# Heads of a gated recurrence as a pipeline of two, and an output product begun with seven of eight tiles

## The reference, cut to what matters

```python
def lru_coeffs(u2, p):                       # per head of 128 channels, two directions
    gr, gi = u @ w_r, u @ w_i                # 128x128 matrices per head and direction
    r, i = sigmoid(gr + b_r), sigmoid(gi + b_i)
    log_a = -8 * r * softplus(-lam)
    return exp(log_a), sqrt(-expm1(2 * log_a)) * (i * u)     # a, bx

def rglru_branch(xb, p, h0):
    u = depthwise_conv(xb, sconv_w, sconv_b)                 # 4 taps
    y = scan forward (h = a*h + bx) + scan backward, both from h0
    return y, last states

def even_mixer(h, h0, p):                    # D_MODEL 1024, 512 positions
    va, vg, ga, xb, gb = split(h @ w_in)
    y_a = silu(layernorm(depthwise_conv(va * sigmoid(vg), 31 taps))) * silu(ga)
    y_b = rglru_branch(xb, p, h0) * silu(gb)
    return concatenate([y_a, y_b]) @ w_out
```

## Time and profile before

| what | value |
|---|---|
| median of 3 runs | 1792.26 us (1791.04 to 1792.68) |
| the profiled execution's own time | 1792.62 us |
| its span, first to last instruction | 1791.3 us |
| PE busy | 1673.2 us (93%) |
| DVE busy | 992.5 us (55%) |
| ACT busy | 746.1 us (42%) |
| share of PE in the chain that ended last | 71%; DVE 14%, ACT 10%, issue 4% |

### The profile page before, as it was taken

The page is one execution under the profiler, slowest core; times in us unless marked ns, Lnnn a source line. Parts: engine busy times, 40 slices in busy tenths (PEclk is TensorE's granted clock), DMA queues, the critical chain, the costliest instruction groups (busy, mean ns, idle before and its releaser), DMA issues.

```text
span 1791.3 us, 19102 instructions
## 1 busy us (share of the span) xinstructions
PE 1673.2 (93%) x7670; PEld 1297.0 (72%) x7670; DVE 992.5 (55%) x1362; ACT 746.1 (42%) x1014; POOL 19.4 (1%) x40
## 2 busy tenths in 40 slices
PE   6798899996997999999799989999999999999996
PEld 4677666664785888888587857776677788888885
DVE  4677768777757556744744453345545544444333
ACT  3567665765434333332334444334433322332221
POOL 0000000000000000000000000000000000000000
PEclk9799999998998999999899989999999999999998
DMA  7345536454231233232132111221122233232321
GB/s 315 117 159 182 190 129 202 150 178 154 71 106 59 94 97 104 91 100 94 46 111 69 67 47 55 77 70 56 62 94 95 83 102 98 95 94 94 106 94 47
DMA packets 55063, 190.46 MB, mean 106 GB/s; under 512 B 7328, under 2 KB 7328, under 8 KB 54720
## 3 DMA queue, kind: packets, MB, share of 16 engines
q1 hardware_dynamic: 47616, 159.52, 27.4%
q0 software_dynamic: 4960, 18.20, 3.1%
q10 hardware_dynamic: 2400, 11.53, 1.6%
HBM read 178.63 MB, written 2.10 MB: 101 GB/s over the span
## 4 chain that ended last, share of the span: by engine, by line
PE 71%; DVE 14%; ACT 10%; issue 4%; ACTq 1%; DMA 0%; DVEq 0%
PE banks L1446 21%; PE banks L1448 21%; PE banks L1447 21%; ACT w_hi L412 2%; PE banks L1693 2%; DVE w_lo L843 2%; DVE u L980 2%; PE banks L1466 1%; ACT aa L504 1%; ACT tr L506 1%; DVE ti L997 1%; DVE tr L1001 1%; DVE tr L1005 1%; ACT tr L499 1%; PE banks L1715 1%
## 5 line engine op out<-in xcount | busy, mean ns | idle before, releaser
L1446 PE MATMUL banks<-h_hi,w_hi 128*128 128x512 f32 x1408 | 561.1, 398 | 24.4 <-DVE h_lo L919 10.3
L1447 PE MATMUL banks<-h_lo,w_hi 128*128 128x512 f32 x1408 | 553.1, 393 | 0.0
L1448 PE MATMUL banks<-h_hi,w_lo 128*128 128x512 f32 x1408 | 552.3, 392 | 0.0
L843 DVE TENSOR_TENSOR w_lo<-raw,w_hi 128x1024 fp32r<-128x1024 f32 x276 | 336.5, 1223 | 295.5 <-ACT w_hi L412 295.1
L412 ACT ACTIVATE w_hi<-raw 128x1024 fp32r<-128x1024 f32 x276 | 288.2, 1050 | 159.2 <-PE banks L1448 147.8
L1446 PEld LDWEIGHTS banks<-h_hi,w_hi 128*128 128x128 f32 x1408 | 266.7, 189 | 102.6 <-issue 34.4
L1448 PEld LDWEIGHTS banks<-h_hi,w_lo 128*128 128x128 f32 x1408 | 267.3, 190 | 56.9
L1447 PEld LDWEIGHTS banks<-h_lo,w_hi 128*128 128x128 f32 x1408 | 267.5, 190 | 53.8 <-issue 0.7
L1446 PE MATMUL banks<-y_hi,w_hi 128*128 128x512 f32 x192 | 76.8, 400 | 5.7 <-ACT gs L716 5.6
L1448 PE MATMUL banks<-y_hi,w_lo 128*128 128x512 f32 x192 | 76.8, 400 | 0.0
L1447 PE MATMUL banks<-y_lo,w_hi 128*128 128x512 f32 x192 | 76.1, 396 | 0.0
(11 more groups left out here) (347 smaller groups left out, 2145.8 us busy)
## 6 DMA issues: line engine op xcount, KB each, us to landing
raw<-weights SPq DMA_DIRECT2D x284, 512.0 KB, 3.5
mraw<-modt POOLq DMA_DIRECT2D x32, 512.0 KB, 4.5
mod<-modw ACTq DMA_DIRECT2D x4, 2048.0 KB, 23.0
rep<-U SPq DMA_DIRECT2D x96, 64.9 KB, 2.7
rep<-U SPq DMA_DIRECT2D x32, 64.8 KB, 2.5
X<-x_in ACTq DMA_DIRECT2D x1, 2048.0 KB, 13.2
out<-X SPq DMA_DIRECT2D x4, 512.0 KB, 2.7
ctx_x<-ctx_in ACTq DMA_DIRECT2D x1, 1024.0 KB, 19.8
```

What stands on the lines that cost most here:

```text
L843: tt(slot(w_lo, c), slot(raw, c), slot(w_hi, c).bitcast(F32), ALU.subtract).then_inc(S["lo"], 1)
L1446: mm(o, wh, r_hi, start=start, stop=False)
L1447: mm(o, wh, r_lo, start=False, stop=False)
L1448: return mm(o, wl, r_hi, start=False, stop=stop)
```

## The change

Roots, scans and outputs of a head move behind the input of the next head. On ACT `head_input` is cut into the copy to `xp` and `head_high` (the split of `u`), `head_roots` of head I-1 stands after the split of the next weight chunk, and the output split is a function of its own. On DVE the order of a main head becomes: the low part of gx, drive of the head before, `convolved`, scans and output of the head before, conv of this head. The first of the two scratch tiles of square roots is no longer `xp` but a part of `yb_lo`'s tile; the context's `u` gets two halves. The 32 conditioning steps are divided as one per context head and three per main head. On PE the first three chunks of yb are begun with seven of the eight tiles, ahead of the sum of `csum` (behind the first), and finished with the eighth afterwards.

```diff
+    o_ybl = p.at
     yb_lo = p("yb_lo", NT * T, F32R)
+    thf = [at(f"thf{i}", T, o_ybl + 2 * K * i) for i in range(NT)]
@@ ACT
-        def head_input(I, w, b):    # xp, then u_hi
+        def head_input(I, w, b):
+            if I: e.wait_ge(S["conv"], I)
+            else: e.wait_ge(S["pad"], 1)
+            fn(xp[:, 2:2 + w], bank(b, w), ACT.Copy).then_inc(S["xp"], 1)
+        def head_high(I, w):
+            e.wait_ge(S["conv"], I + 1)
+            if I: product(gc or gx of head I - 1)
+            fn(u_hi[:, 0:w], u_of(I), ACT.Copy).then_inc(S["uhi"], 1)
@@ ACT, context heads
             head_input(i, TC, 4)
+            head_high(i, TC)
             ahead("vg", i)
+            if i:
+                head_roots(i - 1)
             product("vg", i)
...
             head_gates(i, TC, ...)
-            head_roots(i, TC)
@@ ACT, main heads
             ahead("xb", i)
+            if i:
+                convolved(i - 1)
+            head_roots(NT + i - 1)
             product("xb", i)
             head_input(NT + i, T, 0)
             if i:
-                convolved(i - 1)
+                head_high_out(i - 1)
+            head_high(NT + i, T)
             ahead("gb", i)
...
             ahead("cw", i)
-            head_roots(NT + i, T)
-            e.wait_ge(S["yact"], i + 1)
-            fn(tile(yb_hi, i), u[:, :], ACT.Copy).then_inc(S["ybhi"], 1)
         convolved(NT - 1)
+        head_roots(2 * NT - 1)
+        head_high_out(NT - 1)
@@ DVE, context heads
             ahead("xc", i)
-            head_input(i, TC)
+            if i:
+                head_drive(i - 1, TC)
+            head_conv(i, TC)
             ahead("vg", i)
+            head_low(i, TC)
+            if i:
+                context_scan(i - 1)
             ahead("va", i)
+            conditioning(i)
             e.wait_ge(S["sig"], i + 1)
             product("va", i)
             stt(U ...).then_inc(S["uu"], 1)
             ahead("gc", i)
-            head_drive(i, TC)
-            conditioning(2 * i)
-            head_scan(i, TC, lambda k: 0.0)
-            conditioning(2 * i + 1)
@@ DVE, main heads, after the change
+            ahead("xb", i)
+            head_drive(NT + i - 1, T if i else TC)
+            if i:
+                convolved(i - 1)
+                head_sum(i - 1)        # both scans, their sum, the gate
+            else:
+                context_scan(NT - 1)
+            head_conv(NT + i, T)
+            if i:
+                head_low_out(i - 1)    # yb_lo
+            ahead("gb", i)
+            head_low(NT + i, T)
+            conditioning(NT + 3 * i)
+            stt(tg ...)                # the gate of gb
+            conditioning(NT + 3 * i + 1)
+            ahead("ga", i)
+            ahead("gx", i)
+            conditioning(NT + 3 * i + 2)
+            stt(sga ...)               # the gate of ga
+            ahead("cw", i)
+        head_drive(2 * NT - 1, T)
+        convolved(NT - 1)
+        head_sum(NT - 1)
+        head_low_out(NT - 1)
@@ PE
-        e.wait_ge(S["csum"], NT)
-        feature_sum(0, csum[:, :])
+        def yb_early(f):
+            c = ready("yb", f)
+            if f == 0:
+                e.wait_ge(S["yblo"], NT - 1)
+                e.wait_ge(S["gread"], 2 * NT)
+            blocks(bank(BANK_OF[f]), c, yb_hi, yb_lo, n=KC - 1, stop=False)
+        def yb_late(f):
+            if f == 0:
+                e.wait_ge(S["yblo"], NT)
+            blocks(..., b0=KC - 1, k0=KC - 1, n=1, start=False, stop=False).then_inc(S["mm"], 1)
         for f in range(3):
-            yb(f)
+            yb_early(f)
+            if f == 0:
+                e.wait_ge(S["csum"], NT)
+                feature_sum(0, csum[:, :])
+        for f in range(3):
+            yb_late(f)
         e.wait_ge(S["usum"], NT - 1)
         feature_sum(1, ti[0][:, :])
```

More of the change, by code:

```diff
@@ L124 @@
     "vec x ctx cst cst2 out hi lo mm crep csb mdv v a zero eps pad sil sp_z sp_e wdt rows cols rows_c x_sum x_sq fsum f_sq "
[L125 removed]
+    "norm_t norm_hi norm_lo xp conv uhi ulo gread e2 mv sq scan sig uu "
     "tgt sgb sgat sga cpe csum yact ybhi yblo ymu usum usq yln ysil yga yhi yalo res xsq xsum "
@@ L357, in program, with u_of, th_of @@
     xg = (sqb[:, :], s2[:, :])
+    def u_of(I):
+        return u[:, :] if I >= NT else tile(u, I % 2, TC)
+    def th_of(I, k):
+        return (thf[I % NT], th[1])[k][:, 0:T if I >= NT else TC]
     def sp():
@@ L488, in head_input @@
                 product(*(("gc", I - 1) if I <= NT else ("gx", I - NT - 1)))
-            fn(u_hi[:, 0:w], u[:, 0:w], ACT.Copy).then_inc(S["uhi"], 1)
+            fn(u_hi[:, 0:w], u_of(I), ACT.Copy).then_inc(S["uhi"], 1)
         def head_gates(I, w, gates):
-            if I:
+            if I > NT:
+                e.wait_ge(S["yblo"], I - NT)
+            elif I:
                 e.wait_ge(S["scan"], I)
@@ L530, in convolved, with head_high_out @@
             fn(tile(U, i, T, UW), bank(3), ACT.Identity, bias=cb2[:, i:i + 1]).then_inc(S["cpe"], 1)
+        def head_high_out(i):
+            e.wait_ge(S["yact"], i + 1)
+            fn(tile(yb_hi, i), tr[0][:, :], ACT.Copy).then_inc(S["ybhi"], 1)
         for i in range(NT):
             ahead("xb", i)
+            if i:
+                convolved(i - 1)
+            head_roots(NT + i - 1)
             product("xb", i)
@@ L983, in head_input, with head_low @@
             m.then_inc(S["conv"], 1)
+        def head_low(I, w):
             e.wait_ge(S["uhi"], I + 1)
-            low(u_lo[:, 0:w], u[:, 0:w], u_hi[:, 0:w]).then_inc(S["ulo"], 1)
+            low(u_lo[:, 0:w], u_of(I), u_hi[:, 0:w]).then_inc(S["ulo"], 1)
         def head_drive(I, w):
@@ L989, in head_drive @@
                 e.wait_ge(S["e2"], 2 * I + k + 1)
-                stt(th[k][:, 0:w], tr[k][:, 0:w], 1.0, th[k][:, 0:w], ALU.add, ALU.mult).then_inc(S["mv"], 1)
-                own.did(stt(ti[k][:, 0:w], ti[k][:, 0:w], 1.0, u[:, 0:w], ALU.add, ALU.mult))
+                stt(th_of(I, k), tr[k][:, 0:w], 1.0, th_of(I, k), ALU.add, ALU.mult).then_inc(S["mv"], 1)
+                own.did(stt(ti[k][:, 0:w], ti[k][:, 0:w], 1.0, u_of(I), ALU.add, ALU.mult))
         def head_scan(I, w, init):
@@ L996, in head_scan, with context_scan @@
                 own.wait()
[L997 to L1006, removed]
+                own.did(tt(ti[k][:, 0:w], ti[k][:, 0:w], th_of(I, k), ALU.mult))
+                own.wait()
+                way = slice(None, None, 1 - 2 * k)
+                own.did(e.tensor_tensor_scan(tr[k][:, 0:w][:, way], aa[k][:, 0:w][:, way], ti[k][:, 0:w][:, way], init(k), ALU.mult, ALU.add))
+            own.wait()
+        def context_scan(i):
+            head_scan(i, TC, lambda k: 0.0)
+            for k in range(2):
+                m = e.tensor_copy(ctx_state[:, 2 * i + k:2 * i + k + 1], tr[k][:, (TC - 1, 0)[k]:(TC, 1)[k]])
+                m.then_inc(S["scan"], 1) if k else own.did(m)
         for i in range(NT):
             ahead("xc", i)
-            head_input(i, TC)
+            if i:
+                head_drive(i - 1, TC)
+            head_conv(i, TC)
             ahead("vg", i)
+            head_low(i, TC)
+            if i:
+                context_scan(i - 1)
             ahead("va", i)
+            conditioning(i)
             e.wait_ge(S["sig"], i + 1)
@@ L1029, in convolved, with head_sum, head_low_out @@
             tt(csum[:, :], csum[:, :], tile(U, i, T, UW), ALU.add).then_inc(S["csum"], 1)
+        def head_sum(i):
+            head_scan(NT + i, T, lambda k: ctx_state[:, 2 * i + k:2 * i + k + 1])
+            own.did(tt(tr[0][:, :], tr[0][:, :], tr[1][:, :], ALU.add))
+            e.wait_ge(S["sgb"], i + 1)
+            own.wait()
+            stt(tr[0][:, :], tr[0][:, :], 0.5, tg[:, :], ALU.mult, ALU.mult).then_inc(S["yact"], 1)
+        def head_low_out(i):
+            e.wait_ge(S["ybhi"], i + 1)
+            low(tile(yb_lo, i), tr[0][:, :], tile(yb_hi, i)).then_inc(S["yblo"], 1)
         for i in range(NT):
             ahead("xb", i)
-            head_input(NT + i, T)
+            head_drive(NT + i - 1, T if i else TC)
             if i:
                 convolved(i - 1)
+                head_sum(i - 1)
[4 more added lines that the diff above has]
+                head_low_out(i - 1)
             ahead("gb", i)
+            head_low(NT + i, T)
+            conditioning(NT + 3 * i)
             e.wait_ge(S["tgt"], i + 1)
             stt(tg[:, :], tg[:, :], 1.0, bank(1), ALU.add, ALU.mult).then_inc(S["sgb"], 1)
+            conditioning(NT + 3 * i + 1)
             ahead("ga", i)
             ahead("gx", i)
+            conditioning(NT + 3 * i + 2)
             e.wait_ge(S["sgat"], i + 1)
             stt(tile(sga, i), tile(sga, i), 1.0, bank(0), ALU.add, ALU.mult).then_inc(S["sga"], 1)
-            head_drive(NT + i, T)
-            conditioning(2 * (NT + i))
             ahead("cw", i)
[L1046 to L1054, removed]
+        head_drive(2 * NT - 1, T)
         convolved(NT - 1)
+        head_sum(NT - 1)
```

(8 more changed lines are left out.)

19 lines of the change are left out of this document (7 added, 12 removed).

## The result

The changed kernel takes 1817.93 us (median of 4 runs, 1817.38 to 1819.97) against 1792.47 for the kernel before in the same series: a ratio of 1.0142, 95% interval 1.0129 to 1.0154. It is 25 us slower. The forecast was 1812, in a range of 1800 to 1824.

What follows compares the result with a forecast made beforehand. PE, 93% busy, was the bound, with ACT/DVE loops pacing the context and DVE's chain the tail. Second sum 8.9 later, slow start 2.8, clock 7.7: 19.4 added to 1792.6, 1812 us on the median's scale, range 1800 to 1824.

Steps and rivals of the forecast that it cites:

- the slow start of the second sum: Tail: PE restarts at lower clock after some 13 us of waiting, slowing the sum's pair and nine products, 2.8 us.
- Part 1 and 2: Context heads: first gate product 2.1 us later, then 0.96 gained per head; first main round begins 3.5 earlier.
- The loop: Context heads: the chain through ACT, DVE and PE takes 17.16 us a head against 18.12.
- Round 0: First main round: begins 3.5 us earlier, at 209.7, and lasts 28.0 as PE's work.
- Part 3: Main heads: chain waits for gx's transfer, gate product 19.64 us into the round; 29.62 a head against 27.71.
- rival B: Main heads: gx landing grows to 7.2 us, total 1835, or mean 5.2, total 1818; chance 0.15.
- Part 4: Main heads: PE's 3.2 us waits lower its clock in most heads, 1.1 us a head, 7.7 in all.
- Part 5: Conditioning and tail: third conditioning free at 4.5 us landing; round 7 to second sum 60.9 us, tail gains 0.5.
- The third conditioning: Main heads: its transfer lands near 25.5 us into the round, no cost; half a microsecond late at 7.2 landing.
- The new output order: Tail: PE's early yb products save nothing; the wait moves behind the yb chunks, some 13 us before the second sum.
- A: Rival, main heads: same loop but PE's clock holds, total 1804 us; chance 0.17.
- C: Rival, main heads: head does not wait for the landing, rounds 26.5 us, total 1782; chance 0.07.

Runs made afterwards that it cites:

- Experiment 5: Changed kernel plus twelve unread 512-column products on PE between ga and gx of main heads 1 to 7: 1804.34 us, ratio 1.0066.
- experiment 3: Changed kernel with PE's output product back in the order of the kernel before: 1814.91 us, ratio 1.0121.
- experiment 4: Kernel before with only PE's new output product order (three yb chunks begun early, finished later): 1797.76 us, ratio 1.0032.
- experiment 1: Changed kernel with the high and low split of the gx chunk moved back behind the head's roots, scans and conv: 1778.64 us, ratio 0.9922.
- experiment 2: Changed kernel moving and splitting only the 512 columns of gate chunks gc and gx that hold matrices: 1778.72 us, ratio 0.9923.

## Why the prediction was right

The direction, the mechanism and most terms held; the time came out 6 us above the forecast, inside the range. These 6 us are a sum of errors of both signs. Clock in rounds 1 to 6: 5.0 too little. Late landings: 2.4 not counted. The stretch behind the output product: 1.4 more, in code that is the same. Against these, round 1 began 1.6 earlier than forecast, for the 1.7 us ahead of the heads, and the slow start of the second sum cost 1.3 less. That about a third of the errors cancels is luck, so each term is judged by itself below.

*Part 1 and 2, context.* Forecast 2.1 later at the first gate product; 80.94 became 81.37 with all before it 1.66 earlier, so 2.1. The loop: forecast 17.16, measured 17.07. Round 0: forecast 3.5 earlier, measured 5.8, of which 1.7 lies ahead of the heads: 4.1. Right to 0.6.

*Part 3, the main loop.* Forecast 19.64 from round to gate product; measured 19.57 to 19.89 in five rounds and 20.65 in two. Experiment 5, with the clock held, gives rounds of 29.57 to 29.82 in five of six against 29.62. Right. The landing took about 1 us longer in two of seven rounds (5.3 us at 363.8 against 4.2 at 300.2), some 2.4 us of the total and not the 20 of rival B. The sharing with POOL's transfers, which rival B rests on, does not explain it. POOL's last transfer ahead of the late round at 363.65, and its landing:

```profile
357.63 0.53 POOL L407 DMA_DIRECT2D mraw<-modt  x1 [2.89 <-DVE modcol L926]
...
DMA to landing us min/median/max: 3.8/3.8/3.8
```

It had landed 2.4 us before the gx transfer started at 363.79. In all seven rounds POOL's last one had landed by then, 0.9 to 2.6 us earlier. The Trainium skill, page "DMA: Bandwidth & Descriptors", section "Issuing engines are not separate DMA queues", says that transfers started by different engines run on the same 16 DMA engines; here POOL's and this one were never on the way together. The copies for the convolution that SP starts right behind gx (line 380) follow it in the quick rounds as well. Why two landings were late stays open.

*Part 4, the clock.* This is the mis-sized term. I took five falls of seven and 1.1 us a head, 7.7 in all. It fell in all seven, and gate product to next round grew by 1.5 to 2.8, 1.9 on the mean: 13.1. Experiment 5 took back 11.6 of it in rounds 1 to 6 and 1.0 in round 7. My upper bound of 1.7 a head was too low. It came from one stretch of 3.4 us at half speed, behind a wait of 2.4. In the rounds at 331.08 and 395.85, which lost 2.7 and 2.8, the lower clock went on into cw (0.78 from 355.40 to 359.00, above). The trace of before had such a longer stretch, behind the wait of 4.04 at 80.94:

```profile
80.90:84.50 3.60, 3.56 (x17) 3.59 (x18) 2.98 (x4) 3.38 (x6) 0.00 (x0) 0.50 0.28 75
84.50:88.00 3.50, 3.50 (x21) 3.50 (x21) 1.57 (x4) 3.48 (x7) 0.00 (x0) 0.63 0.88 287
```

There the low clock lasted until 87.05, 6.1 us; a bound worked out from it would have been 3 us a head (an estimate: half of 6.1).

*Part 5, conditioning and the tail.* The third conditioning cost nothing that counts: DVE waited once for such a transfer in the main heads, 0.2 us. Round 7 to the second sum: forecast 60.9 and a clock fall of 1.1, measured 61.9. PE's wait of 12.81 ahead of the second sum is the forecast 13. The slow start behind it cost 1.5, not 2.8: I had charged the sum's own pair and nine products in full. The new output order gains nothing (experiments 3 and 4), but the reason given was not complete. With the old order in the changed kernel the second sum came 1.7 later and the slow start was avoided, which evens out. And in the kernel before the new order also delays ACT by 3.7 us through the place of a chunk.

*Rivals.* A is what experiment 5 makes of the kernel, 1804.3 against 1804; that the totals agree so closely is in part luck, since that execution reached the heads 2.9 us earlier than the one before. C, the faster side, described the kernel of experiment 1: rounds of 26.4 (26.5), total 1778.6 (1782). It needed the landing out of the chain, and that is what that edit does.

## What to carry to other kernels

When work is reordered around a split or a load, ask for each buffer which product frees it and when its transfer can start; an instruction that was hidden by 6 us can become the head of the chain, and in-order engines hold everything behind it. When a stage is a loop, add up its links once with the start distances of the old trace: here the sum was right to 0.1 us in the rounds whose transfer landed after 4.2 to 4.3 us, as assumed. And a wait of PE inside such a loop counts more than its length, since the clock afterwards is in the loop too.

## What the runs showed of the hardware

After waits of PE of 2.9 to 4.0 us the granted clock fell each time: to 0.50 to 0.67 in seven of seven heads of the changed kernel, and to 0.50 to 0.59 in seven of seven of experiment 3. After waits of 1.4 us and less it stayed at 1.00, in the context of the changed kernel (116 to 202 us) and in the main heads of experiment 2. Twelve products that nobody reads, put into each wait, kept it at 1.00 and made the kernel 13.6 us faster, 12 to 13 of them by the clock. A transfer of half the columns, 256 KB, landed after 2.7 to 3.5 us where the whole one took 4.2 to 5.3 in the same place.
